# First loads and operand splits reordered by use in a two-block forward pass, and a value projection split around a recurrence level

## The reference, cut to what matters

```python
def ssd_mixer(u, w_in, conv_w, conv_b, dt_bias, a_log, d_skip, norm_w, w_out):
    zxbcdt = u @ w_in                                   # 1024 -> z 2048, x 2048, B 4*128, C 4*128, dt 32
    z, xbc, dt = jnp.split(zxbcdt, [SSD_D_INNER, SSD_D_INNER + SSD_CONV_DIM], axis=-1)
    xbc = jax.nn.silu(causal_depthwise_conv(xbc, conv_w, conv_b))
    xs, bm, cm = jnp.split(xbc, [SSD_D_INNER, SSD_D_INNER + SSD_BC_DIM], axis=-1)
    dt = jax.nn.softplus(dt.astype(jnp.float32) + dt_bias.astype(jnp.float32))
    a = -jnp.exp(a_log.astype(jnp.float32))
    a_cs = jnp.cumsum(dt * a, axis=2)                   # per chunk of 128 tokens
    cb = jnp.einsum('bclgn,bcsgn->bcgls', cm, bm)
    y_diag = jnp.einsum('bcgls,bcgrls,bcsgrp->bclgrp', cb, decay, xdt)
    ...

def hgrn2_mixer(u, w_in, lb, norm_w, w_out):
    q, fz, v, g = jnp.split(u @ w_in, 4, axis=-1)       # 8 heads of 128
    scores = jnp.einsum('blhk,bshk,blshk->bhls', q_, kk, dec)
    o = jnp.einsum('bhls,bshv->blhv', scores, v_) + jnp.einsum('blhk,bhkv->blhv', q_ * jnp.exp(b_), s_prev)
    ...
```

## Time and profile before

| | |
|---|---|
| median of three runs | 1921.58 us (1920.56 to 1922.81) |
| the profiled execution, its own time | 1922.01 us |
| span of the profile | 1920.2 us |
| VectorE busy | 1119.9 us, 58% |
| ScalarE busy | 925.4 us, 48% |
| mean granted clock of TensorE | 0.995 |
| first x transposes on TensorE | 5.92 to 12.03 us |
| VectorE's first subtraction of x | at 7.66 us |
| SyncE issues the transfer of `w_dt` | at 3.09 us, landed 9.0 us later |
| TensorE waits in the second mixer's seven projecting heads | 3.7 us, all for VectorE's level operand |

### The profile page before, as it was taken

How to read it: one execution, slowest core, us unless ns; L and a number is a source line. 1 busy time by engine, 2 the same in 40 slices (tenths; PEclk the granted TensorE clock), 3 DMA queues, 4 the chain that set the end, 5 groups by cost and what they waited for, 6 DMA issues and landing times.

```text
span 1920.2 us, 27141 instructions
## 1 busy us (share of the span) xinstructions
PE 1881.6 (98%) x9766; PEld 1582.8 (82%) x9766; DVE 1119.9 (58%) x2000; ACT 925.4 (48%) x1835; POOL 175.8 (9%) x137
## 2 busy tenths in 40 slices
PE   7999999999999999999999999999999999999998
PEld 6787887787888888789998977888888879887986
DVE  4577665645443444657777876534444587456765
ACT  4755756335333324446767655424233365435551
POOL 0101102022000000400100004000000120001100
PEclk9999999999999999999999999999999999999999
DMA  6121313414222232213312114322332232320001
GB/s 205 45 66 45 110 45 110 154 66 153 89 88 87 103 115 88 88 45 89 88 44 64 47 66 152 111 88 87 106 112 88 88 100 80 124 100 1 1 0 44
DMA packets 117634, 162.41 MB, mean 85 GB/s; under 512 B 6085, under 2 KB 58147, under 8 KB 117539
## 3 DMA queue, kind: packets, MB, share of 16 engines
q1 hardware_dynamic: 116243, 156.43, 24.5%
q0 software_dynamic: 1296, 4.72, 0.7%
HBM read 159.03 MB, written 2.10 MB: 84 GB/s over the span
## 4 chain that ended last, share of the span: by engine, by line
PE 85%; DVE 6%; ACT 5%; DVEq 2%; issue 1%; ACTq 0%; DMA 0%; SPq 0%
PE psum L902 49%; PE psum L699 16%; PE psum L1076 5%; PE psum L664 5%; PE psum L1109 2%; PE psum L1338 2%; PE psum L848 1%; DVE z_lo L2160 1%; DVE w_lo L2374 1%; DVEq L2638 1%; PE psum L996 1%; ACT w_hi L1786 1%; DVE w_lo L2209 1%; DVE arena L2227 1%; PE psum L843 0%
## 5 line engine op out<-in xcount | busy, mean ns | idle before, releaser
L2374 DVE TENSOR_TENSOR w_lo<-slot,w_hi 128x512 fp32r<-128x512 f32 x304 | 213.7, 718 | 380.0 <-ACT w_hi L1625 379.9
L1625 ACT CAST w_hi<-slot 128x512 fp32r<-128x512 f32 x304 | 184.8, 621 | 432.9 <-PE psum L902 415.2
L902 PE MATMUL psum<-f_lo,w_hi 128*128 128x512 f32 x528 | 206.1, 390 | 0.0
L902 PE MATMUL psum<-f_hi,w_hi 128*128 128x512 f32 x512 | 200.6, 392 | 4.4 <-DVE f_lo L2381 3.8
L902 PE MATMUL psum<-f_hi,w_lo 128*128 128x512 f32 x512 | 199.7, 390 | 0.0
L902 PE MATMUL psum<-w_hi,hid_hi 128*128 128x512 f32 x512 | 199.5, 390 | 0.0
L902 PE MATMUL psum<-w_hi,hid_lo 128*128 128x512 f32 x512 | 199.2, 389 | 0.0
L902 PE MATMUL psum<-w_lo,hid_hi 128*128 128x512 f32 x512 | 199.2, 389 | 0.0
L2981 POOL TENSOR_TENSOR res<-rn,gb 128x1024 f32<-128x1024 f32 x16 | 43.7, 2732 | 854.1 <-DVE rn L2362 854.1
L902 PEld LDWEIGHTS psum<-f_hi,w_hi 128*128 128x128 f32 x512 | 96.5, 188 | 26.0 <-DVE f_lo L2381 4.6
L902 PEld LDWEIGHTS psum<-f_lo,w_hi 128*128 128x128 f32 x528 | 99.6, 189 | 20.8 <-issue 0.2
(11 more groups left out here) (374 smaller groups left out, 4371.1 us busy)
## 6 DMA issues: line engine op xcount, KB each, us to landing
slot<-in_w_mlp SPq DMA_DIRECT2D x128, 512.0 KB, 5.7
slot<-in_w_ssd SPq DMA_DIRECT2D x32, 512.0 KB, 5.6
slot<-in_w_hgrn SPq DMA_DIRECT2D x32, 512.0 KB, 6.7
slot<-in_w_ssd_out SPq DMA_DIRECT2D x16, 512.0 KB, 6.1
slot<-in_w_gate SPq DMA_DIRECT2D x16, 512.0 KB, 5.3
gb<-in_w_ssd SPq DMA_DIRECT2D x8, 512.0 KB, 8.2
slot<-in_w_hgrn_out SPq DMA_DIRECT2D x8, 512.0 KB, 5.5
slot<-in_w_mla SPq DMA_DIRECT2D x8, 512.0 KB, 5.2
```

Of the source, the lines that this page charges most:

```text
L902: m = pe.matmul(psum[:, bank[c], cols or slice(0, width)], a, m_, start=opens and k == 0 and n_pass == 0, stop=closes and k == KD - 1 and ...
L1625: act.copy(w_hi[:, k, :], as_k(slot_of(stage, n))[:, k, :]).then_inc(high_made, 1)
L2374: dve.tensor_tensor(w_lo[:, k, :], as_k(slot_of(stage, n))[:, k, :], w_hi[:, k, :].bitcast(F32), ALU.subtract).then_inc(low_made, 1)
```

## The change

What it does: `w_dt` is handed over as its 32 columns alone, packed so that each partition reads one run of 1 KB, and is loaded before x's fourth tile; its high part is one cast and its low part one subtraction, placed before x's fourth tile on both engines, into operands that VectorE clears at the start. TensorE waits before the dt product for the half tiles that it needs. The parameter tables are transposed into banks 6 and 7. The split of x01 of group 0 stands directly behind that of B and C. In group 0 the masking of CB stands before the z split and the taps of x2. In the second mixer the first token tile's value projection stands between levels 2 and 3.

```diff
-        wdt = xw[:].rearrange("p t d -> p (t d)")[:, 0:KD * P].rearrange("p (k n) -> p k n", k=KD)
+        wdt = xw[:].rearrange("p t d -> p (t d)")[:, KD * P:KD * P + KD * S_HEADS].rearrange("p (k n) -> p k n", k=KD)
...
-        banks.stage("start", [("par", 0), ("par_b", 1)] + [(("x", t, h), 2 + (2 * t + h) % 4) for t in range(NT) for h in range(2)])
+        banks.stage("start", [("par", 6), ("par_b", 7)] + [(("x", t, h), 2 + (2 * t + h) % 4) for t in range(NT) for h in range(2)])
...
             for t in range(NT):
+                if t == NT - 1:
+                    sp.dma_start(wdt, w_dt.rearrange("p (k n) -> p k n", k=KD)).then_inc(sig("wdt_in"), 16)
                 sp.dma_start(x_rows[:, t, :], x[t * P:(t + 1) * P, :]).then_inc(x_in[t], 16)
-            sp.dma_start(wdt, w_dt.rearrange("(k p) n -> p k n", p=P)).then_inc(sig("wdt_in"), 16)
...
-            wait_features("start", lambda t, h: ("x", t, h))
+            pe.wait_ge(sig("wdt_low"), 1)
             b = claim("dt", "dt")
             for k in range(KD):
-                if k % 2 == 0:
-                    pe.wait_ge(sig("wdt_low"), k // 2 + 1)
+                if k % 4 == 0:
+                    for t in range(NT):
+                        wait_taken(pe, "start", ("x", t, k // 4))
...
                     hgrn_project(*nxt, 0)
                     hgrn_project(*nxt, 1)
                     hgrn_level(par, i, 2)
+                    hgrn_project(*nxt, 2, range(1))
                     hgrn_level(par, i, 3)
                     if not first:
                         hgrn_turn(h - 1)
-                    hgrn_project(*nxt, 2)
+                    hgrn_project(*nxt, 2, range(1, 2))
                     hgrn_level(par, i, 4)
...
                     act.copy(in_hi[:, 4 * h:4 * h + 4, t * P:(t + 1) * P], by_block(psum[:, b, :])).then_inc(sig("x_high"), 1)
-            act.wait_ge(sig("wdt_in"), 16)
-            for n in range(4):
-                act.copy(wdt_hi[:, 2 * n:2 * n + 2, :], wdt[:, 2 * n:2 * n + 2, :]).then_inc(sig("wdt_high"), 1)
+                if t == NT - 2:
+                    act.wait_ge(sig("wdt_in"), 16)
+                    act.wait_ge(sig("wdt_cleared"), 1)
+                    act.copy(wdt_hi[:, :, DT_ROW:P], wdt).then_inc(sig("wdt_high"), 1)
...
             ssd_high(0, "bc")
+            ssd_high(0, "x01")
...
-            ssd_high(0, "x01")
             ssd_high(0, "x23")
...
+            dve.memset(wdt_hi[:].bitcast(F32), 0.0)
+            dve.memset(wdt_lo[:].bitcast(F32), 0.0).then_inc(sig("wdt_cleared"), 1)
             for t in range(NT):
+                if t == NT - 1:
+                    dve.wait_ge(sig("wdt_high"), 1)
+                    dve.tensor_tensor(wdt_lo[:, :, DT_ROW:P], wdt, wdt_hi[:, :, DT_ROW:P].bitcast(F32),
+                                      ALU.subtract).then_inc(sig("wdt_low"), 1)
...
-            for n in range(4):
-                dve.wait_ge(sig("wdt_high"), n + 1)
-                ks = slice(2 * n, 2 * n + 2)
-                dve.tensor_tensor(wdt_lo[:, ks, :], wdt[:, ks, :], wdt_hi[:, ks, :].bitcast(F32),
-                                  ALU.subtract).then_inc(sig("wdt_low"), 1)
...
+            ssd_low(0, "x01")
             dve.wait_ge(ssd_small_in, 48)
...
             dve.tensor_tensor(decay_end, tot, acs, ALU.subtract).then_inc(sig("sums_ready"), 1)
-            ssd_low(0, "x01")
             ssd_low(0, "x23")
...
-                ssd_low(g, "z")
-                taps(4, ("x", 2), 4 * g + 2)
-                b = full(stage, "CB")
-                dve.tensor_tensor(CBm, by_block(psum[:, b, :]), tri.unsqueeze(1).broadcast_to([P, NT, P]), ALU.mult)\
-                    .then_inc(bank_free[b], 1)
...
+                if g == 0:
+                    masked_cb()
+                    ssd_low(g, "z")
+                    taps(4, ("x", 2), 4 * g + 2)
+                else:
+                    ssd_low(g, "z")
+                    taps(4, ("x", 2), 4 * g + 2)
+                    masked_cb()
```

More of the change, by code:

```diff
@@ L2254, in ssd_group, with masked_cb @@
                 taps(3, ("x", 1), 4 * g + 1)
-                ssd_low(g, "z")
-                taps(4, ("x", 2), 4 * g + 2)
-                b = full(stage, "CB")
-                dve.tensor_tensor(CBm, by_block(psum[:, b, :]), tri.unsqueeze(1).broadcast_to([P, NT, P]), ALU.mult)\
-                    .then_inc(bank_free[b], 1)
+                def masked_cb():
+                    b = full(stage, "CB")
+                    dve.tensor_tensor(CBm, by_block(psum[:, b, :]), tri.unsqueeze(1).broadcast_to([P, NT, P]), ALU.mult)\
+                        .then_inc(bank_free[b], 1)
+                if g == 0:
[6 more added lines that the diff above has]
+                    masked_cb()
                 dve.drain()
@@ L3067 @@
         "x": a["x"][0], "p": a["p"][:, 0], "cst": shape_constants(), "par_a": conv, "par_b": par_b,
-        "w_ssd": a["ssd_w_in"][0], "w_dt": a["ssd_w_in"][0][:, S_DT - DT_ROW:], "dt_bias": a["ssd_dt_bias"][0],
+        "w_ssd": a["ssd_w_in"][0], "w_dt": a["ssd_w_in"][0][:, S_DT:].reshape(KD, P, S_HEADS).transpose(1, 0, 2).reshape(P, KD * S_HEADS), "dt_bias": a["ssd_dt_bias"][0],
         "a_log": a["ssd_a_log"][0], "d_skip": a["ssd_d"][0], "w_ssd_out": a["ssd_w_out"][0], "w_hgrn": a["hgrn_w_in"][0],
```

## The result

| | before | changed kernel |
|---|---|---|
| median of five runs of each on one chip | 1922.17 us (1920.56 to 1922.81) | 1911.66 us (1911.02 to 1912.08) |
| the profiled execution, its own time | 1922.01 us | 1911.02 us |
| span of the profile | 1920.2 us | 1909.2 us |
| mean granted clock of TensorE | 0.995 | 0.997 |

The ratio is 0.9947 with a 95% interval of 0.9936 to 0.9957: 10.5 us less, 0.53%, against a bound of 0.2% for what can be told from no change. Forecast were 10.9 us less.

What follows compares the result with a forecast made beforehand. TensorE, busy 98% of the span, was taken as the bound, with gains only in its waits and half clock; 7.0 us in the first mixer plus 3.9 in the heads made 10.9, from 1921.6 to 1910.7 us, range 1908.9 to 1915.6.

Steps and rivals of the forecast that it cites:

- The dt product: Start of the kernel: TensorE starts the dt product at 13.5 instead of 14.17, worth 0.65 us.
- The clock of the dt product: Stretch behind the start of the dt product: full clock is kept instead of 0.54, worth 1.6 us, or nothing.
- Block B: Start: with the parameter tables in banks 6 and 7, the wait for bank 0 goes, 0.91 us.
- x01: Group 0: four of eight x subtractions behind the decay sums leave the chain to the silu of x0, 2.45 us.
- masked CB: Group 0: TensorE's 1.74 us wait for bank 4 goes, 0.4 us is given back at bank 7.
- The new waits: Group 0, TensorE: some 0.5 us at the transposes of x0 for the silu, about 0.4 us for bank 7.
- The heads: Second mixer: level 3's wait goes, level 6's operand limits the gain to 0.65 us in six heads, 3.9 us.
- (1): Rival at the dt product: clock falls as before, 9.3 us gained, 1912.3 us; chance 0.30.
- (2): Rival in the second mixer: level 3's gain is waited away at levels 5 and 6, 1914.6 us; chance 0.12.
- (3): Rival at the start: slot 0 lands late and softplus waits behind x01's casts, at worst 1915.1 us; chance 0.05.
- Rival 4: Second mixer: level 3's result comes too late for VectorE, delaying level 6 six times, slower, 1926.3 us; chance 0.02.
- Rival 5: Start: the change doesn't do what it says, for instance VectorE's chain moves under 2 us, 1915.7 us; chance 0.04.

## Why the prediction was right

**The sum.** 10.9 us forecast, 10.5 measured by the medians, 11.0 by the two profiled executions. It splits as predicted: 7.0 us in the first mixer and 3.8 in the heads by the traces; 6.4 and 3.9 by the medians with the heads' part taken away. The mechanism is right in every term but the clock's, where the reason given was not shown; some sizes missed in opposite directions.

**The dt product.** Forecast start 13.5, measured 13.63, with the order of subtractions as worked out. As a clock time this is partly luck: in the changed kernel and its variants the start lies between 13.63 and 14.60, and the run of before with only the heads changed has 13.62. Two things move it, when x lands and when TensorE first comes to full clock. The rows of the x transposes with their mean ns, in after and in the run with the keys' copy moved, between 10.3 and 12 us:

```profile
L665 PE MATMUL psum<-con,rn 128*128 128x128 f32 x15 | 2.1, 280 | 0.0
```

```profile
L665 PE MATMUL psum<-con,rn 128*128 128x128 f32 x10 | 2.3, 421 | 0.0
```

In the second run the transposes are still slow there and end later, so VectorE gets its half tiles 0.85 us apart and the dt product starts at 14.58. For the same reason the pause before the product, 0.72 to 1.55 us in the new order against 2.15 and 2.20 in the old, does not measure what the change takes off. Counted from VectorE's first subtraction of x's second tile it does show: 3.83 us in after and mostly 4.33 in its variants, 4.45 and 4.81 in the old order, and, at equal pace, 4.33 against 4.93 when TensorE waits for all half tiles. So the 0.65 us is right as a difference at equal pace (0.6), not as two clock times; between the two profiles it was 0.54.

**The clock of the dt product.** The forecast took it as kept, and in all eleven profiles of the changed kernel and its variants it was, behind pauses of 0.72 to 1.77 us. In three of them, though, all x transposes still took 421 ns, so that full clock came only as they ended or within the pause, and these say little about a pause letting it fall. And the reason given for it, full transposes on the near side of the pause, is not shown: the old order has them too, and there the clock fell behind 2.15 us in one profile and stayed behind 2.20 in another. The price of 1.6 us (3.6 x 0.46 is nearer to 1.7; 1.54 measured) was compared with the one execution of before in which it fell. It is the weakest term: in the two profiles it is real, in the medians it can be worth less, which may account for the first mixer's 6.4 instead of 7.0. How much of it is the change's doing stays open.

**Block B, x01, CB.** For block B 0.91 was forecast, the idle time in the row; its start came 1.13 us sooner in the trace, since without the wait it also overlaps the two transposes before it, and the run with the tables put back lost 1.1 us by the trace and 0.7 to 1.0 by the medians. That the start of B came 3.2 us sooner as forecast (0.65 + 1.6 + 0.91) is therefore a sum of 0.54, 1.54 and 1.13, whose misses cancel. For x01 2.45 was forecast and 2.3 measured; for the masked CB 1.3 net and about 1.3 in the trace. The new waits stand where they were named, 0.48 us for the silu of x0 (0.5 forecast) and 0.40 for bank 7 (0.4), and the silu came 5.65 us sooner. The chain over VectorE and ScalarE was the right thing to follow: counting TensorE's own idle and half clock would have promised 6.2 us where 5.65 came.

**The heads.** Level 3's wait went, and the stretch from level 2 to level 4 is 7.98 us, 0.91 less where 0.8 was forecast. The forecast then let level 6's operand cut this to 0.65 in every head. It does so only in part: level 6 starts 0.89 us behind level 5 where nothing holds it, in heads 5 and 6, 1.09 to 1.18 in heads 1, 3 and 4, and 1.36 in head 2, with 0.30 us of wait. The periods of the heads shrink by 0.34 us in head 2 and by 0.53 to 0.78 in the others, 3.7 in all or 0.62 a head. So the average is as forecast, while the limit that was to set it binds clearly in one head of six. VectorE's wait in head 0 is 1.12 us, 1.3 forecast, and the head's period of 30.4 us is as before.

**The rivals.** The clock did not fall (1), the level wait did not merely move (2), the x01 split was not in the way (3): slot 0's cast could start at 21.62 and its last subtraction ended at 24.8, before the dt transposes' result was taken at 25.73. Rival 4 did not happen, because level 3's result was there before VectorE took it at 950.48. The whole projection between the levels shows that its mechanism is real, and roughly at its price: level 3 starts 2.9 us later there, the room in after is about 1.4 us (947.99 + 1.06 to 950.48) where 1.1 was forecast, so a head should lose 1.5 us, and the seven projecting heads lose 1.7 each on average. Rival 5 is out, as the first mixer gave 7.0 us.

## What to carry to other kernels

Where an engine stands still for an operand, follow the chain that makes the operand, not the idle time: moving work of another engine from ahead of the chain to behind it pays what it takes off the chain, and the wait shows up again, shorter, at the next meeting point. A block of independent work set between two dependent steps hides their wait as long as its length stays below the other engine's room for the later result; one block of 3 us was right here and two cost 11.8 us. And before a stretch of half clock is booked as a gain, look at it in more than one execution. At the start of a kernel, where the landing of loads and the first rise of the clock shift all later work by up to 1 us from run to run, measure a change from an event behind them, not from the start of the span.

## What the runs showed of the hardware that was not expected

TensorE's clock after a short pause is not settled by the pause. Behind 1.46 us of idle before block x0 the granted clock fell to half (0.72 over the six us from 36) in before and in the run with the heads alone, and stayed at 1.00 in the run with x01 late and in the one with the filled pause. Before the dt product it fell behind 2.15 us and stayed behind 2.20. By the Trainium skill, page "TensorE: Matmul & The Clock Gate", section "Why this matters for your kernels", none of these is long enough for the clock to fall; the traces contradict it in three of these six cases. What decides between them stays open. Each such stretch costs about 1.7 us (12 us at 0.86), and their number seems to go with the spread of the runs: in the groups above, the executions of before with a mean clock of 0.996 have spans of 1918.2 to 1920.0 us, those at 0.995 spans of 1919.5 to 1922.5 us. Two more places return. All fourteen profiles, before and after, have such a stretch between 1173 and 1194 us, each time behind a pause of TensorE of 3.4 to 3.8 us, and there trace and page agree. Twelve have one between 1115 and 1133 us, after three pauses close together (0.78, 1.32 and 0.49 us in after), and the two that lack it have such pauses too.

TensorE does not start at full clock, and the moment of its rise moves. The x transposes take 421 ns each at first and 272 ns later; in after they change in x's third tile, in three variants the last one still takes 421 ns, although the same instructions stand there. x's tiles do not land alike from run to run either: TensorE's transposes began between 5.02 and 6.36 us, and in eleven of the fourteen profiles it stood still a second time, for 0.44 to 1.06 us near 8 us, before x's second tile. Both together move the start of the dt product by up to 1 us with the same order of work, which is as much as one of the smaller parts of this change.
